# Neighbourhood attention: the projection of a head pair in sixteen like pieces, and the values' transposes in the next pair's first slot

## The reference, cut to what matters

```python
q_l, k_l, v_l = jnp.split(h_lat @ w_qkv, 3, axis=-1)      # 512 tokens
q_c, k_c, v_c = jnp.split(h_ctx @ w_qkv, 3, axis=-1)      # 256 tokens; q_c is not used here
...
s_nb = (q_r . k in its window) + bias                     # 8 x 16 neighbours
s_cx = jnp.einsum('bchd,blhd->bhcl', q_r, k_c)
p = softmax(concatenate([s_nb, s_cx]))
o = p_nb . v_win + p_cx . v_c
```

## Time and profile before

| | us |
|---|---|
| median of 3 runs | 4178.53 |
| the profiled execution | 4184.53 |
| its span | 4182.5 |
| first to last product of `na_h` with `na_w` | 1270.4 to 1598.7 |

### The profile page before, as it was taken

The page is one execution under the profiler, slowest core; times in us unless marked ns, Lnnn a source line. Parts: engine busy times, 40 slices in busy tenths (PEclk is TensorE's granted clock), DMA queues, the critical chain, the costliest instruction groups (busy, mean ns, idle before and its releaser), DMA issues.

```text
span 4182.5 us, 52761 instructions
## 1 busy us (share of the span) xinstructions
PE 3833.2 (92%) x21504; PEld 2995.4 (72%) x21504; DVE 1851.6 (44%) x2839; ACT 1319.7 (32%) x1950; POOL 459.4 (11%) x379
## 2 busy tenths in 40 slices
PE   7889989999997998999888898899998898889999
PEld 3555657888885887788766666688876666767887
DVE  3556544434334344444533455543333445554333
ACT  4334333313123333323324321232233433124222
POOL 1221201000012120000211220000021122000000
PEclk9999999999998999999999999999999999999999
DMA  5223421211211322222121210233222121113322
GB/s 195 83 90 111 127 95 43 70 61 61 68 49 61 106 71 91 81 95 97 57 55 38 79 46 26 67 93 100 91 67 60 33 75 46 31 50 100 101 91 71
DMA packets 327713, 317.04 MB, mean 76 GB/s; under 512 B 8944, under 2 KB 314000, under 8 KB 327344
## 3 DMA queue, kind: packets, MB, share of 16 engines
q1 hardware_dynamic: 327472, 313.68, 24.0%
HBM read 311.55 MB, written 2.10 MB: 75 GB/s over the span
## 4 chain that ended last, share of the span: by engine, by line
PE 80%; DVE 11%; ACT 4%; issue 2%; POOL 1%; DMA 1%; DVEq 0%; SPq 0%; ACTq 0%; POOLq 0%
PE PS L133 79%; DVE scr L147 5%; ACT scr L143 2%; DVE scr L157 1%; DVE scr L165 1%; DVE PS L161 1%; PE PS L136 1%; ACT L143 1%; DVE NBt L157 1%; DVE scr L169 1%; POOL ring_r L147 1%; DVE scr L177 0%; ACT NBt L143 0%; DVE scr L153 0%; POOL NBt L147 0%
## 5 line engine op out<-in xcount | busy, mean ns | idle before, releaser
L133 PE MATMUL PS<-scr 128*128 128x128 f32 (+7 forms) x7124 | 659.0, 284 | 124.8 <-DVE scr L147 65.0
L133 PEld LDWEIGHTS PS<-scr 128*128 128x128 f32 (+3 forms) x7124 | 512.8, 155 | 268.7 <-issue 103.2
L133 PE MATMUL PS<-ffn_h,ffn_w 128*128 128x512 f32 (+1 forms) x3168 | 616.1, 357 | 7.9 <-DVE ffn_h L157 5.7
L133 PEld LDWEIGHTS PS<-ffn_h,ffn_w 128*128 128x128 f32 x3168 | 524.6, 189 | 100.5 <-issue 9.1
L143 ACT ACTIVATE scr<-PS 128x256 f32<-128x256 f32 (+4 forms) x405 | 187.6, 463 | 740.7 <-PE PS L133 682.2
L133 PE MATMUL PS<-h_h,ring_r 128*128 128x512 f32 (+1 forms) x976 | 357.5, 429 | 38.5 <-POOL ring_r L147 24.6
L133 PE MATMUL PS<-mlp_h,mlp_w 128*128 128x512 f32 x1536 | 361.3, 396 | 0.0
L143 ACT ACTIVATE scr<-scr 128x256 f32<-128x256 f32 (+5 forms) x392 | 194.9, 497 | 524.7 <-DVE scr L157 322.4
L133 PE MATMUL PS<-mlp_g,mlp_w 128*128 128x512 f32 x1536 | 359.7, 396 | 0.0
L133 PEld LDWEIGHTS PS<-mlp_h,mlp_w 128*128 128x128 f32 x1536 | 288.4, 188 | 70.4 <-issue 1.0
L133 PEld LDWEIGHTS PS<-mlp_g,mlp_w 128*128 128x128 f32 x1536 | 288.5, 188 | 69.9
(11 more groups left out here) (153 smaller groups left out, 4739.6 us busy)
## 6 DMA issues: line engine op xcount, KB each, us to landing
ring<-in_ffn_w_in SPq DMA_DIRECT2D x44, 1024.0 KB, 5.0
scr<-in_ada_w SPq DMA_DIRECT2D x52, 768.0 KB, 4.8
ring<-in_w_up SPq DMA_DIRECT2D x32, 1024.0 KB, 5.5
ring<-in_w_down SPq DMA_DIRECT2D x32, 1024.0 KB, 5.3
ring<-in_w_in SPq DMA_DIRECT2D x60, 512.0 KB, 3.9
ring<-in_ffn_w_out SPq DMA_DIRECT2D x16, 1024.0 KB, 5.2
scr<-in_na_bias SPq DMA_DIRECT2D x32, 512.0 KB, 5.1
ring<-in_na_w_qkv SPq DMA_DIRECT2D x24, 512.0 KB, 4.1
```

Source lines behind the costliest of these rows:

```text
L133: return self.eng.matmul(o, lhsT=l, rhs=r, start=start, stop=stop) if self.eng else Nothing()
```

## The change

The sixteen pieces are cut anew and put in another order. For each pair from the second on the background of the turns begins with all nine transposes of the pair whose turns are just beginning (`turned(tl - 1)` in `project(tl)`), one piece; then queries 4 pieces, latent keys 4, context keys 2, latent values 4, context values 1. A piece of 512 columns is two k-steps, of context keys four, the context values are one piece of eight. A ninth background, `project(8)`, has the transposes of the last pair. The first projection, ahead of the turns, has no transposes in it.

On ACT the copy of the context values moves to the first slot of the next pair (`values_in(tl - 1, 1)`; only for the first pair it stays at the end of the first projection), the three copies to `VX` go into that pair's second slot, and the copies of queries and keys come one slot after their last product. The rounding of the next pair's queries' and keys' weights comes behind the copy of the context keys. The work on DVE is the same and in the same order; SP and POOL keep theirs too, with POOL's second rounding one slot later.

```diff
@@ -1712,7 +1712,7 @@
         scores(0)
         for it, (tl, m) in enumerate(na_work):
             if m == 0:
-                bg = project(tl + 1) if tl < 7 else iter(())
+                bg = project(tl + 1)
             spread(it)
             if it + 1 < len(na_work):
                 scores(it + 1)
...
@@ -1767,48 +1765,40 @@
             pe.mm(o, wh[:, k, :], nhl[:, k, c], False, False)
             return pe.mm(o, wl[:, k, :], nhh[:, k, c], False, k == 7)
 
-        def qk(tl, parts):
-            for what, j, (t0, tn) in parts:
-                o_ = 0 if what == "q" else 1024
-                wh, wl = w8(o_, 1024), w8(2048 + o_, 1024)
-                o, before = cur["rg"].take("na_made", "n_in", tl, j)
-                emptied(pe, before)
-                for k in range(8):
-                    pe.wait_ge(*at("nl", "na", k, int(t0 == 0)))
-                    t = three(o[:, 0:tn], wh, wl, slice(t0, t0 + tn), k)
-                    if k == 7:
-                        t.then_inc(*pe.up("na_in_full", "n_full", tl, j))
-                    if k == 3:
-                        yield
-                yield
-
-        def project(tl):
-            pe.wait_ge(*at("na_lo", "qk", tl))
-            yield from qk(tl, NQK[:2])
-            wh, wl = w8(4096, 1024), w8(5120, 1024)
-            pe.wait_ge(*at("na_lo", "v", tl))
-            for s, (t0, tn) in enumerate(LC):
-                o, before = cur["rg"].take("na_made", "n_vt", tl, s)
-                emptied(pe, before)
-                for k in range(8):
-                    pe.wait_ge(*at("nl", "na", k, s))
-                    t = three(o[:, 0:tn], wh, wl, slice(t0, t0 + tn), k)
-                    if k == 7:
-                        t.then_inc(*pe.up("na_in_full", "nv_full", tl, s))
-                    if k == 3:
-                        yield
-                yield
-            yield from qk(tl, NQK[2:])
+        def product(tl, name, full, wh, wl, t0, tn, per):
+            o, before = cur["rg"].take("na_made", *name)
+            emptied(pe, before)
+            for k in range(8):
+                pe.wait_ge(*at("nl", "na", k, int(t0 == 0)))
+                t = three(o[:, 0:tn], wh, wl, slice(t0, t0 + tn), k)
+                if k == 7:
+                    t.then_inc(*pe.up("na_in_full", *full))
+                if k % per == per - 1:
+                    yield
+
+        def turned(tl):
+            pe.wait_ge(*at("na_made", "n_vt", tl, 1))
             for g in range(3):
                 o, before = cur["rg"].take("na_made", "n_vx", tl, g)
                 emptied(pe, before)
-                pe.wait_ge(*at("na_made", "n_vt", tl, 1))
                 for c in range(3):
                     v = V_AT[3 * g + c]
                     t = pe.tr(o[:, c * 128:c * 128 + 128], VT[:, v:v + 128], ident)
                 t.then_inc(*pe.up("na_in_full", "nvx_full", tl, g))
-                yield
-                yield
+
+        def project(tl):
+            if tl:
+                turned(tl - 1)
+                yield
+            if tl == 8:
+                return
+            pe.wait_ge(*at("na_lo", "qk", tl))
+            for (what, j, (t0, tn)), per in zip(NQK, (2, 2, 4)):
+                o_ = 0 if what == "q" else 1024
+                yield from product(tl, ("n_in", tl, j), ("n_full", tl, j), w8(o_, 1024), w8(2048 + o_, 1024), t0, tn, per)
+            pe.wait_ge(*at("na_lo", "v", tl))
+            for s, (t0, tn) in enumerate(LC):
+                yield from product(tl, ("n_vt", tl, s), ("nv_full", tl, s), w8(4096, 1024), w8(5120, 1024), t0, tn, (2, 8)[s])
 
         def scores(it):
             tl, m = na_work[it]
@@ -1861,39 +1851,43 @@
         split_act("qk", 0)
         norm_act(act, "na", LC, ada_gain(1, 0, f_col)[1], na_parts)
 
-        def qk(tl, what, j, t0, tn):
-            yield
-            act.wait_ge(*at("na_in_full", "n_full", tl, j))
-            if tl >= 2:
-                act.wait_ge(*at("ns_full", 4 * (tl - 2) + 3))
-            act.f(QT[tl % 2] if what == "q" else KTt[tl % 2][:, t0:t0 + tn], psum("na_made", "n_in", tl, j)[:, 0:tn], ACT.Copy,
-                  scale=64 ** -0.5 if what == "q" else 1.0).then_inc(*act.up("na_made", "n_in", tl, j))
-            yield
+        def values_in(tl, s):
+            t0, tn = LC[s]
+            act.wait_ge(*at("na_in_full", "nv_full", tl, s))
+            if tl:
+                act.wait_ge(*at("na_in_full", "nvx_full", tl - 1, 2))
+            act.f(VT[:, t0:t0 + tn], psum("na_made", "n_vt", tl, s)[:, 0:tn], ACT.Copy).then_inc(*act.up("na_made", "n_vt", tl, s))
 
         def project(tl):
-            u = tl % 2
-            split_act("v", tl)
-            for what, j, (t0, tn) in NQK[:2]:
-                yield from qk(tl, what, j, t0, tn)
-            for s, (t0, tn) in enumerate(LC):
-                yield
-                act.wait_ge(*at("na_in_full", "nv_full", tl, s))
-                if tl:
-                    act.wait_ge(*at("na_in_full", "nvx_full", tl - 1, 2))
-                act.f(VT[:, t0:t0 + tn], psum("na_made", "n_vt", tl, s)[:, 0:tn], ACT.Copy).then_inc(*act.up("na_made", "n_vt", tl, s))
-                yield
-            what, j, (t0, tn) = NQK[2]
-            yield from qk(tl, what, j, t0, tn)
+            if tl > 1:
+                values_in(tl - 1, 1)
+            if tl < 8:
+                split_act("v", tl)
+            if tl:
+                yield
+                for g in range(3):
+                    act.wait_ge(*at("na_in_full", "nvx_full", tl - 1, g))
+                    if tl >= 3:
+                        act.wait_ge(*at("no_full", 4 * (tl - 3) + 3))
+                    act.f(VX[(tl - 1) % 2][:, 3 * g:3 * g + 3, :], psum("na_made", "n_vx", tl - 1, g)[:, 0:384].rearrange("p (c e) -> p c e", c=3),
+                          ACT.Copy).then_inc(*act.up("na_made", "n_vx", tl - 1, g))
+            if tl == 8:
+                yield
+                return
+            for (what, j, (t0, tn)), n in zip(NQK, (4, 4, 2)):
+                yield from idles(n)
+                act.wait_ge(*at("na_in_full", "n_full", tl, j))
+                if tl >= 2:
+                    act.wait_ge(*at("ns_full", 4 * (tl - 2) + 3))
+                act.f(QT[tl % 2] if what == "q" else KTt[tl % 2][:, t0:t0 + tn], psum("na_made", "n_in", tl, j)[:, 0:tn], ACT.Copy,
+                      scale=64 ** -0.5 if what == "q" else 1.0).then_inc(*act.up("na_made", "n_in", tl, j))
             if tl < 7:
                 split_act("qk", tl + 1)
-            for g in range(3):
-                yield
-                act.wait_ge(*at("na_in_full", "nvx_full", tl, g))
-                if tl >= 2:
-                    act.wait_ge(*at("no_full", 4 * (tl - 2) + 3))
-                act.f(VX[u][:, 3 * g:3 * g + 3, :], psum("na_made", "n_vx", tl, g)[:, 0:384].rearrange("p (c e) -> p c e", c=3),
-                      ACT.Copy).then_inc(*act.up("na_made", "n_vx", tl, g))
-                yield
+            yield from idles(4)
+            values_in(tl, 0)
+            yield
+            if tl == 0:
+                values_in(tl, 1)
 
         def scores(it):
             z = it % 2
...
```

More of the change, by code:

```diff
@@ L1742, in project @@
             fetch()
-            for _ in range(6):
-                yield
+            yield from idles(6)
             fetch()
-            for _ in range(10):
-                yield
+            yield from idles(10)
         def scores(it):
@@ L1965, in project @@
         def project(tl):
+            if tl == 8:
+                return
             split_pool("v", tl)
-            for _ in range(10):
-                yield
+            yield from idles(11)
             if tl < 7:
                 split_pool("qk", tl + 1)
-            for _ in range(6):
-                yield
+            yield from idles(5)
         na_turns(project, idle, idle, idle, idle)
```

## The result

The changed kernel takes 4217.4 us (median of 5 runs). One of the five, 4503.52, was disturbed and is in no comparison; the other four lie between 4209.35 and 4220.0. The forecast was 4212, with a range of 4196 to 4223. The ratio of the undisturbed runs to those of the kernel before (4178.53) is 1.0083, 95% interval 1.0069 to 1.0097: 35 us slower, where +33.6 was forecast. The profiled execution took 4217.4 us with a span of 4215.3, 32.8 more than before. The attention stage holds nearly all of it: from its first product to the first product of the next stage it takes 1668.99 - 1270.62 = 398.4 us, and took 1636.61 - 1270.39 = 366.2.

The account below looks back on a forecast made before the run. PE was taken to bound pairs 0 to 6. Start +3.6, heads +15.5, pair 6's waits -2.3, last pair +4.2, clock +12.6 give +33.6 us on 4178.5: forecast 4212, range 4196 to 4223.

Parts of the forecast that it names:

- from there to the last pair's row of values and scores: Six heads +15.5 us, pair 6's lost waits -2.3, half clock behind the heads +11.1.
- from there to the next stage: Last pair: transposes wait at its head and delay flip and values, +4.2 us, plus 1.5 for half clock.
- What goes: PE's waits between flip and values for DVE's copy out of PSUM vanish in pairs 0 to 6: 2.34 us a pair.
- the bank's wait: First product behind a head's transposes waits for the first copy to VX to free its PSUM bank: 0.74 us.
- The head: Transposes wait for scores, maxima, exponentials, copy: 4.18 us idle, 4.92 with the bank; net +2.58 a pair, +15.5 for six.
- The clock: PE falls to half clock for 5.2 us behind each head's idle time: 1.85 us a head, +12.6 with the last pair.
- slow transposes: Nine transposes at half speed at a head end 0.25 us behind the first copy to VX.
- The start: First product of the turns waits for a copy to VX behind four exponentials and a rounding: 1321.25 against 1317.63, +3.6 us.
- The clock stays up: Rival, chance 0.24: transposes break the heads' idle time in two, so PE keeps full clock; 4199.5 us.
- down for long: Rival, chance 0.05: some 12 us of half clock a head, 5.5 us lost each for six; 4235 us.
- Not filled: Rival, chance 0.04: new pieces too short to fill the gaps behind flip; 4228 us.
- The faster case: Rival, chance 0.04: waits behind flip go and PE stays fed through the heads; 4165.7 us.

Follow-up runs that it names:

- e1_early: Changed kernel with ACT alone reordered: at a pair's head, context-values copy and copies to VX before the two exponentials, weights' rounding behind; 4161.8 us, ratio 0.9961.
- e3_busy: Changed kernel with sixteen extra matmuls of 512 columns, results overwritten, in PE's idle time at heads of pairs 1 to 7; 4203.9 us, ratio 1.0064.
- e2_copy: Changed kernel with only ACT's copy of the context values moved back to the end of its own pair; 4209.0 us, ratio 1.0078.
- e0_after: The changed kernel measured again without any edit; 4209.7 us, ratio 1.0079.
- e5_start: Changed kernel with context-values copy and VX copies before the exponentials at the first pair only, values' weights' rounding behind VX copies everywhere; 4203.3 us, ratio 1.0065.
- e4_copy_split: Changed kernel with the context-values copy back in its own pair and the values' weights' rounding behind the copies to VX on ACT; 4197.2 us, ratio 1.0050.

## Why the prediction was right

By its own steps, in microseconds between the two profiled executions:

| stretch | forecast | measured |
|---|---|---|
| to the first product of the turns (from the stage's first) | +3.6 | 51.39 - 47.24 = +4.15 |
| from there to the last pair's row of values and scores | +15.5 - 2.3 + 11.1 = +24.3 | 312.02 - 289.96 = +22.1 |
| from there to the next stage | +4.2 + 1.5 = +5.7 | 34.96 - 29.02 = +5.9 |
| sum | +33.6 | +32.2 |

**What goes.** Right: no wait behind flip is left in pairs 0 to 6. e1_early shows what it is worth where nothing takes its place: 41.50 - 39.70 = 1.80 a pair. Of that some 0.25 are paid back in the bank's wait (transposes to product 1.22 us there, 0.97 without a wait by the forecast), so the gaps give about 2.05, against the 2.34 forecast. The idle times that the rows record are 0.45 + 1.57 = 2.02 a pair, which is near it. The forecast let PE be free 0.33 us behind the start of three transposes, where their row lasts 0.49; that this makes up the 0.29 between is likely, not shown.

**The head.** Right in mechanism and nearly in size: 4.08 us of recorded idle time, the chain of the forecast link by link. At full clock the head costs 4.80 over e1_early (e3_busy), and 4.80 - 1.80 = 3.00 a pair over the kernel before, against 2.58. That the bank's wait stands right behind is shown by e2_copy, where removing the first wait alone gained nothing.

**The clock.** The term that was mis-sized: 1.85 a head was forecast, 1.08 measured (e3_busy against the changed kernel). I took 5.2 us of half clock from the start of the transposes, 3.5 of them on products, by two gaps of 4.30. From the product to where PEclk goes back to 1.00 it is 2.4, 1.1, 3.9, 1.9, 0.9 and 3.8 us (the windows shown, to within 0.2), 2.35 on average, and 0.46 x 2.35 = 1.08. In e0_after the same count gives 2.54 on average, so 1.17, and 45.70 - 44.50 = 1.20 were measured. The price per microsecond was right, the length was not, and the 0.25 us for slow transposes wasn't there: they lie beside ACT's rounding and copy (1.85 us from transposes to product, 1.86 in e3_busy at full clock). The forecast took one length, from two other places in the program, for all heads; it is not the same from head to head. This excess of 4.6 over six heads was made up in part by the gaps and the head at full clock, 0.4 a pair (2.5 over six) the other way. So the sum is closer than its terms, and that much is luck: with the clock's term alone at its measured size, the forecast would have been +29.0.

**The start.** +4.15 instead of +3.6. The chain was as forecast, 10.64 us from the scores (1311.37) to the product, 10.95 forecast. But the last copy of the first projection came 40.3 us behind the stage's first product instead of 39.4. Windows of the two kernels, the changed one first:

```profile
1294.00:1296.00 2.00, 2.00 (x6) 1.54 (x6) 0.00 (x0) 0.00 (x0) 0.17 (x1) 0.53 0.19 43
```
```profile
1294.00:1296.00 2.00, 2.00 (x11) 1.62 (x10) 0.00 (x0) 0.00 (x0) 0.00 (x0) 1.00 0.32 87
```

The same products at half clock for 2 us longer: 0.46 x 2 = 0.9. In e5_start this stretch was again short (its last product ends 39.4 us behind the first). The seven traces with the new order, whose first projection has the same instructions, bear this out: from the stage's first product to the first scores it is 39.8 us in e5_start and 40.5 to 41.1 in the other six, and the clock comes back 23.3 us behind that product in e5_start and 24.6 to 26.0 in the others. So the same instructions give both, by when the clock came back in the run. Of the kernel before there is one trace (23.5 us), so whether the change shifts this too stays open.

**The rivals.** "The clock stays up" falls by the windows; "down for long" too. "Not filled" falls by the waits. The faster case, given 0.04, falls by the heads' waits; e1_early shows that it was one reordering on ACT away, at 4162, near the 4165.7 that this rival named.

## What to carry to other kernels

When work moves into a gap of one engine, look on the engine that feeds it for what now stands ahead of the feeding instruction: here a copy of 0.38 us, and the copies to VX after it, came to stand behind two exponentials of the turn that PE had only just begun, and that cost 4.8 us at full clock at each of six heads, where the filled gaps gave 2 a pair. Before taking away a wait that a trace names, look for the next wait on the same engine; e2_copy removed 28.6 us of recorded waiting and gained nothing. The mend here was an order on the engine that was waited for (short copies that free a bank or feed a transpose first, long work with slack behind), not a move of the matmuls.

## What the runs showed of the hardware that I had not expected

An idle time of 3.1 us between dense products was followed by half clock at all six heads of e4_copy_split, and it set in 0.7 to 1.3 us after the work was back. The same idle time may cost nothing or 3.2 us at half clock (2.15 us at the start, e5_start and e1_early), so a price for one such place is known only on average; over six like heads it was 0.8 to 3.8 us. The Trainium skill (TensorE: Matmul & The Clock Gate, "Why this matters for your kernels") warns of idle gaps between bursts of matmuls. The traces agree for 3.16 us (e4_copy_split) and 4.08 us (changed kernel). Filling such a gap with matmuls whose result is thrown away gave back 1.08 us a head (e3_busy).
